# The sparse keys as the last column tile, with the local bias strip in their room and two sets of local rows

## The reference

```python
h = rms_norm(x, ln_attn_pre[l])
mix = hybrid_mixer(h, w_in[l], ...)          # proj = h @ w_in, then three families of heads
x = x + rms_norm(mix @ w_out[l], ln_attn_post[l])
h = rms_norm(x, ln_ffn_pre[l])
f = (jax.nn.silu(h @ ffn_w_gate[l]) * (h @ ffn_w_up[l])) @ ffn_w_down[l]
x = x + rms_norm(f, ln_ffn_post[l])
```

```python
logits = einsum(q, k) / sqrt(d) + bias_tab[t5_bucket(dist)]
p = where(mask, exp(logits - m), 0); out = (p / denom) @ v
```

## Time and profile before

| what | value |
| --- | --- |
| median of 3 runs (lowest to highest) | 1344.51 us (1343.56 to 1347.97) |
| profiled execution | 1344.31 us, its span 1342.4 us |
| mean granted TensorE clock | 0.982 |
| busy over the span | PE 96%, DVE 58%, ACT 41%, POOL 13% |
| DMA | 120.69 MB, mean 90 GB/s |
| value products | to about 72 us |
| first pieces | to about 138 us |
| stick-breaking, local, sparse stage | 138 to 286, to 378, to about 540 us |
| output projection, feed-forward | 549 us to the end |

### The profile page before, as it was taken

One profiled execution on the slowest core, in us unless ns is written; L12 is line 12 of the kernel. 1 busy time (PEld: TensorE's weight loads), 2 busy tenths in 40 slices (PEclk: granted clock), 3 DMA queues, 4 the chain that ended last, 5 costly groups with the idle time before them and its releaser, 6 DMA issues.

```text
span 1342.4 us, 18803 instructions
## 1 busy us (share of the span) xinstructions
PE 1290.8 (96%) x6956; PEld 1104.4 (82%) x6956; DVE 776.7 (58%) x1433; ACT 555.7 (41%) x1044; POOL 177.3 (13%) x162
## 2 busy tenths in 40 slices
PE   7999999989989999799889999999999999999998
PEld 6988788879979999688768888888888778888887
DVE  4342678748757664556856655665566554444455
ACT  4322677747656544433543333333333331121131
POOL 1000000000000000011033323332333100000012
PEclk9999999999989999899989999999999999999999
DMA  7013411134251110522222222212221352332343
GB/s 267 1 46 117 122 48 32 44 105 110 67 130 33 35 62 1 173 94 79 79 79 79 79 86 87 93 64 87 87 94 63 118 181 94 100 103 74 104 153 126
DMA packets 58385, 120.69 MB, mean 90 GB/s; under 512 B 7560, under 2 KB 29328, under 8 KB 58294
## 3 DMA queue, kind: packets, MB, share of 16 engines
q1 hardware_dynamic: 58294, 119.48, 28.4%
HBM read 82.73 MB, written 19.95 MB: 76 GB/s over the span
## 4 chain that ended last, share of the span: by engine, by line
PE 53%; DVE 3%; ACT 1%; issue 1%; POOL 1%; DMA 1%; DVEq 0%; SPq 0%; ACTq 0%; POOLq 0%
PE ps L1975 30%; PE ps L1998 17%; PE ps L1917 5%; PE ps L2135 1%; DVE f_topL L1758 0%; DMA ring<-in_ffn_w_gate 0%; DVE o_tmp L1703 0%; DVE f_W L1764 0%; POOL o_rs L1522 0%; DVE ring L1707 0%; PE ps L1905 0%; DMA ring<-in_ffn_w_up 0%; PE ps L2098 0%; POOL e_tail L2089 0%; ACT o_junk L1563 0%
## 5 line engine op out<-in xcount | busy, mean ns | idle before, releaser
L1975 PE MATMUL ps<-f_topH,f_W 128*128 128x512 f32 x704 | 224.4, 395 | 6.3 <-DVE f_W L1764 4.1
L1975 PEld LDWEIGHTS ps<-f_topH,f_W 128*128 128x128 f32 x704 | 134.3, 191 | 35.7 <-DVE f_W L1764 4.9
L1764 DVE TENSOR_TENSOR f_W<-ring,f_W 128x512 fp32r<-128x512 f32 (+1 forms) x122 | 121.6, 1009 | 51.7 <-ACT f_W L1590 51.7
L1590 ACT CAST f_W<-ring 128x512 fp32r<-128x512 f32 (+1 forms) x122 | 72.4, 595 | 164.9 <-PE ps L1998 153.9
L1975 PE MATMUL ps<-f_topL,f_W 128*128 128x512 f32 x352 | 139.0, 395 | 0.0
L893 PE MATMUL ps<-V,m_tw 128*128 128x66 f32 (+1 forms) x1056 | 130.3, 273 | 0.0
L893 PEld LDWEIGHTS ps<-V,m_tw 128*128 128x128 f32 x1056 | 128.1, 194 | 1.1
L1998 PE MATMUL ps<-f_topH,f_W 128*128 128x512 f32 x448 | 125.0, 390 | 0.0
L1975 PE MATMUL ps<-f_headH,f_W 128*128 128x512 f32 x352 | 115.3, 390 | 1.5 <-DVE f_W L1764 1.5
L1764 DVE TENSOR_TENSOR f_W<-f_scr,f_W 128x512 fp32r<-128x512 f32 x88 | 63.5, 723 | 89.9 <-ACT f_W L1590 89.9
L1880 DVE TENSOR_TENSOR QT<-ps,QT 128x1024 f32<-128x1024 f32 (+1 forms) x48 | 50.2, 1047 | 103.6 <-PE ps L1998 103.6
(11 more groups left out here) (236 smaller groups left out, 2556.4 us busy)
## 6 DMA issues: line engine op xcount, KB each, us to landing
m_qs<-m_qn SPq DMA_DIRECT2D x128, 128.0 KB, 2.4
ring<-in_ffn_w_gate SPq DMA_DIRECT2D x22, 512.0 KB, 4.5
ring<-in_ffn_w_up SPq DMA_DIRECT2D x22, 512.0 KB, 3.6
act_kept<-QT SPq DMA_DIRECT2D x44, 256.0 KB, 2.0
f_scr<-act_kept SPq DMA_DIRECT2D x22, 512.0 KB, 3.5
ring<-in_ffn_w_down SPq DMA_DIRECT2D x32, 256.0 KB, 3.5
ring<-in_w_in_tiles SPq DMA_DIRECT2D x13, 512.0 KB, 3.8
ring<-in_ffn_w_down SPq DMA_DIRECT2D x24, 192.0 KB, 2.4
```

What stands on the lines that cost most here:

```text
L1590: act.copy(slots[s % W_RING][:, 0, 0:n], source(s)).then_inc(hi_done, 1)
L1764: dve.tensor_tensor(slots[s % W_RING][:, 1, 0:n], source(s), slots[s % W_RING][:, 0, 0:n].bitcast(F32), ALU.subtract).then_inc(lo_done, 1)
L1975: ins = pe.matmul(ps[:, bank, :], whole[:, w, cols], halves[h][:, k0 + k, col:col + HALF], start=(begins and k == 0 and w == 0 and h == 0) ...
```

## The change

1. The sparse key tile moves behind the two sparse query tiles and is now the last column tile.
2. `strip_swa` lies in the first half of `KSa`, the room of the sparse keys. Its load has no need in the plan any more; in the code it waits for the compression's products and the value products. The copy of the first half of the sparse key tile waits for the last local logits.
3. `rows_swa` has two sets of rows, by the parity of the token tile, in the room of `rows_sb`. The writers of tiles 0 and 1 wait for the last stick-breaking turn, those of later tiles for the turn of the tile two before.
4. `strip_full` lies in the room of `KSb`. Its three loads wait for the last stick-breaking scores. The gain of the sparse family gets a strip item of its own (4), after the last piece.
5. Sparse logits wait for the last piece, window and selection scores for the key tile's half that they read. Sparse queries need the last query tile only.
6. In `values`, the next tile is turned after step 3 in place of 4.

```diff
@@ -47,7 +47,7 @@
 T_TILES += [("q", 2 + i, [(SQ + 128 * i, 128)]) for i in range(4)]
-T_TILES += [("k", 0, [(KSL, 64), (KW, 64)]), ("q", 0, [(NQ, 128)]), ("q", 1, [(NQ + 128, 128)])]
+T_TILES += [("q", 0, [(NQ, 128)]), ("q", 1, [(NQ + 128, 128)]), ("k", 0, [(KSL, 64), (KW, 64)])]
 NTT = len(T_TILES)
@@ -103,6 +103,7 @@
 GROUPS = 4 * NT
+DB = {"swa": 2}
 FAMILY_WIDTH = {"sb": 256, "swa": 512, "nsa": 256}
@@ -156,7 +157,8 @@
             self.first_row[jobs[j].group] = 4 * j
-        self.same_kind_before = [max((k for k in range(j) if (jobs[k].kind, jobs[k].strip) == (jobs[j].kind, jobs[j].strip)), default=None)
+        self.same_kind_before = [max((k for k in range(j) if jobs[k].n <= jobs[j].n - DB.get(jobs[j].kind, 1)
+                                      and (jobs[k].kind, jobs[k].strip) == (jobs[j].kind, jobs[j].strip)), default=None)
                                  for j in range(self.NJ)]
@@ -219,6 +221,7 @@
 
+    last_swa = ("logits", lay.c_sm[lay.chunk0[4 * (SB_JOBS + SWA_JOBS)]] - 1)
     for i in range(FIRST_LOADS, NTT):
@@ -234,7 +237,8 @@
         if s % 4 == 3:
-            add(("half_keep", h), "act", act(HALF) if kind == "q" else 2 * act(HALF), [("piece", s)], -100)
+            add(("half_keep", h), "act", act(HALF) if kind == "q" else 2 * act(HALF),
+                [("piece", s), last_swa if h == 2 * (NTT - 1) else None], -100)
             if kind == "k":
@@ -248,16 +252,17 @@
 
-    add(("strip", 0), "dma", 7000, [("turn", lay.last_turn(SB_JOBS - 1))], -100)
+    add(("strip", 0), "dma", 7000, [], -100)
     for i in range(1, 4):
-        add(("strip", i), "dma", (0, 5000, 5000, 7000)[i], [("piece", PIECES - 1)], -100)
+        add(("strip", i), "dma", (0, 5000, 5000, 7000)[i], [("scores", lay.chunk0[4 * SB_JOBS] - 1)], -100)
+    add(("strip", 4), "dma", 3000, [("piece", PIECES - 1)], -100)
 
 ...
             half = 1 if job.n >= NT // 2 else 0
-            last_tile = {"sb": 4, "swa": job.q_tile + 5, "nsa": NTT - 1}[job.family]
+            last_tile = {"sb": 4, "swa": job.q_tile + 5, "nsa": NTT - 2}[job.family]
             ready = ("half_keep", 2 * last_tile + half) if 2 * last_tile + half >= FIRST_HALVES else None
@@ -265,13 +270,16 @@
         used = ("turn", lay.last_turn(before)) if before is not None else None
+        if job.family == "swa" and job.n < 2:
+            used = ("turn", lay.last_turn(SB_JOBS - 1))
+        keys = ("half_lo", 2 * (NTT - 1) + (job.n >= NT // 2)) if job.kind in ("win", "slc") else None
         for r in range(4 * j, 4 * j + 4):
 ...
                 w = lay.width(c)
-                add(("scores", c), "pe", 2 * pe(w) + (112 if job.kind in ("sb", "win") else 0), [("spread", g), emptied(c - S_SLOTS)], age - 35)
+                add(("scores", c), "pe", 2 * pe(w) + (112 if job.kind in ("sb", "win") else 0), [("spread", g), emptied(c - S_SLOTS), keys], age - 35)
             if job.kind == "sb":
@@ -286,7 +294,8 @@
                     strip = ("strip", 0) if job.kind == "swa" else ("strip", 1 if job.n < 2 else 2 if job.n < 4 else 3)
-                    add(("logits", lay.c_sm[c]), "dve", dve(w), [("scores", c), used, strip], age)
+                    rows_free = ("piece", PIECES - 1) if job.family == "nsa" else None
+                    add(("logits", lay.c_sm[c]), "dve", dve(w), [("scores", c), used, strip, rows_free], age)
                 add(("softmax", lay.n_sm[r]), "act", act(n, 60), [("logits", lay.c_sm[chunks[-1]])], age + 1)
@@ -413,7 +422,12 @@
             blk = sb("blk", [P, 2, 16, NC_CMP], F32, early)
-        KS = [sb("KSa", [P, 4, S], F32R), sb("KSb", [P, 4, S], F32R)]
+        KSa = sb("KSa", [P, 4, S], F32R)
+        with ExitStack() as early:
+            KSb = sb("KSb", [P, 4, S], F32R, early)
+        strip_full = sb("strip_full", [P, 4, S])
+        KS = [KSa, KSb]
+        strip_swa = KSa[:, 0:2, :].bitcast(F32).rearrange("p a (h l) -> p (a h) l", l=SWA_L)
         identr, mask_sb, mask_win = (sb(n, [P, P], F32R) for n in ("identr", "mask_sb", "mask_win"))
@@ -424,7 +438,7 @@
             rows_sb = sb("rows_sb", [P, 4, S], F32, early)
-        strip_swa, rows_swa = sb("strip_swa", [P, 8, SWA_L]), sb("rows_swa", [P, 8, SWA_L])
+        rows_swa = sb("rows_swa", [P, 2, 8, SWA_L])
 
@@ -453,7 +467,6 @@
             wH, wL = sb("wH", [P, W_ITEMS, HALF], F32R, early), sb("wL", [P, W_ITEMS, HALF], F32R, early)
-        strip_full = sb("strip_full", [P, 4, S])
         rows_nsa = {"slc": sb("rows_slc", [P, 4, S]), "win": sb("rows_win", [P, 4, WIN_BLOCKS * P]), "cmp": sb("rows_cmp", [P, 4, 64])}
@@ -546,7 +559,7 @@
             if job.kind == "swa":
-                return rows_swa[:, i + job.strip, cols]
+                return rows_swa[:, job.n % 2, i + job.strip, cols]
             return rows_nsa[job.kind][:, i, cols]
@@ -565,6 +578,8 @@
                 eng.wait_ge(turned, lay.last_turn(before) + 1)
+            elif jobs[r // 4].kind == "swa":
+                eng.wait_ge(turned, lay.last_turn(SB_JOBS - 1) + 1)
 
@@ -660,17 +675,20 @@
                         sp.dma_start(g_w[:], bass.AP(grp_g.tensor, 256, [[0, P], [1, 512]])).then_inc(gains_in[1], 16)
-                        sp.wait_ge(turned, lay.last_turn(SB_JOBS - 1) + 1)
+                        sp.wait_ge(phi_done, NPHI)
+                        sp.wait_ge(v_done, NT)
                         sp.wait_ge(tab_out, 32)
-                        sp.dma_start(strip_swa[:], bass.AP(table_swa.tensor, 0, [[1, P], [SWA_T, 8], [1, SWA_L]])).then_inc(strips_in[0], 16)
+                        sp.dma_start(strip_swa, bass.AP(table_swa.tensor, 0, [[1, P], [SWA_T, 8], [1, SWA_L]])).then_inc(strips_in[0], 16)
+                    elif i == 4:
+                        sp.wait_ge(piece_done, PIECES)
+                        sp.dma_start(g_n[:], bass.AP(grp_g.tensor, 0, [[0, P], [1, 256]])).then_inc(gains_in[2], 16)
                     else:
 ...
                         if i == 1:
-                            sp.wait_ge(piece_done, PIECES)
+                            sp.wait_ge(tab_out, 32)
+                            sp.wait_ge(scores_ready, chunk0[4 * SB_JOBS])
                         sp.dma_start(strip_full[:, :, c0:c1],
                                      bass.AP(table_full.tensor, c0, [[1, P], [FULL_T, 4], [1, c1 - c0]])).then_inc(strips_in[i], 16)
-                        if i == 1:
-                            sp.dma_start(g_n[:], bass.AP(grp_g.tensor, 0, [[0, P], [1, 256]])).then_inc(gains_in[2], 16)
 
@@ -736,7 +754,7 @@
                                                 start=(k == 0 and h is hH and w == 0), stop=(k == KT - 1 and h is hL))
-                        if k == 4 and t + 1 < NT:
+                        if k == 3 and t + 1 < NT:
                             turn_x(t + 1)
@@ -815,8 +833,8 @@
                             pe.wait_ge(half_lo_done, lo_before(2 * 5 + 2))
-                        else:
-                            pe.wait_ge(half_lo_done, lo_before(HALVES))
+                    if job.kind in ("win", "slc"):
+                        pe.wait_ge(half_lo_done, lo_before(HALVES) - (job.n < NT // 2))
                     if c < S_SLOTS:
@@ -933,6 +951,8 @@
                     act.wait_ge(piece_done, 4 * h + 4)
+                    if h == 2 * (NTT - 1):
+                        act.wait_ge(neg_ready, c_sm[chunk0[4 * (SB_JOBS + SWA_JOBS)]])
                     hf, src = h % 2, ps[:, half_bank(h), :]
@@ -1184,6 +1204,8 @@
                         minus_sink()
+                    if job.family == "nsa":
+                        dve.wait_ge(piece_done, PIECES)
                     dve.wait_ge(strips_in[0 if job.kind == "swa" else 1 if job.n < 2 else 2 if job.n < 4 else 3], 16)
```

## The result

The changed kernel takes 1349.53 us (median) beside 1345.29 us for the kernel before: ratio 1.0028 (95%: 1.0017 to 1.0038). A second comparison gave 1348.04 beside 1346.53 us, ratio 1.0011 (0.9997 to 1.0025). So the change costs 1.5 to 4.2 us where the forecast was -5.2, and both medians lie above the range. The second interval takes in no change; that the kernel is slower at all rests on the first. The profiled execution's span is 1346.5 us (1342.4 before).

A forecast was written before the change was run, and what follows sets the result against it. TensorE, busy 96% of the span, was taken as the bound, so only its idle time and low clock could go. Terms -2.4 + 4.4 - 4.3 + 2.0 - 3.1 - 1.8 = -5.2 us took 1344.31 to 1339.1 us, range 1333.5 to 1345.5.

The forecast's parts named there:

- Value products: Value products: turning the next tile one step earlier removes six waits of 0.40 us, -2.4 us (bounds -1.2 and -3.3).
- Front of the SyncE queue: Before stick-breaking: gain and strip delay the first spread 3.8 us, plus 0.6 of low clock, +4.4 us.
- upper bound of +5.4: Upper bound of the front-of-queue term, with up to 1.5 us more for low clock; its lower bound was 0.
- The delay of 2.7 us: First spread's delay if strip and spread were served side by side, sharing the DMA engines, instead of in ring order.
- Stick-breaking to local: Start of the local stage: the 2.8 us idle and 1.5 us of low clock behind it go, -4.3 us.
- the last rival: Near 291 us: the strip's move alone brings nothing, the tile order closes the gap; within the forecast, no chance given.
- The double rows: Local stage: two sets of rows costed at nothing, since VectorE waited for scores before it wrote a row.
- Sparse key tile at the end: End of the local stage: the wait between key halves comes back half covered, +2.0 us (bounds 0 and +4.3).
- Start of the sparse stage: First sparse logits: 0.6 of 3.7 us idle stays, -3.1 us, with a further -1.8 us for the clock.
- The clock's part (-1.8): Start of the sparse stage: less low clock after the shorter idle time, -1.8 us, taken between 0 and -4.2.
- To the end of the kernel: Stages after the sparse one: they keep their work and their order; no term in the sum.
- The rival "given back": Whole kernel: front costs 5.4, key gap uncovered at 4.3, sparse start's clock stays low; 1344.2 us, chance 0.25.

The follow-up runs named there:

- 2: Kernel before the change with only the turn of the next tile after step 3 in place of 4: ratio 0.9983 to the kernel before.
- run 1: Changed kernel with the local strip and gain loads moved from the queue's front to behind the first five spreads: ratio 0.9986 to the kernel before.
- run 3: Kernel before with only the local gain and an unread copy of the 1 MB strip loaded ahead of the first spread: ratio 1.0065, +8.8 us.
- run 8: Changed kernel with gain and strip behind the third spread and the key tile's first half early: 1335.02 and 1335.40 us, ratios 0.9928 and 0.9931 to before.
- 5: Changed kernel with only half of the strip and the gain ahead of the first spread, the other half behind four stick-breaking jobs: ratio 1.0007 to before.
- 6: Changed kernel with one set of local rows in place of two: ratio 1.0021 to the kernel before.
- run 9: Kernel before with only the order of the column tiles changed (sparse keys last), strips and local rows where they were: ratio 0.9994 to the kernel before.
- 4: Changed kernel with 16 unread matmuls of 512 columns on TensorE while it waits for the first spread: ratio 1.0003 to the kernel before.
- run 7: On top of run 1, four pieces of the sparse key tile's first half run ahead of the last local weighings: ratio 0.9953 to the kernel before.

## Why the prediction was wrong

**Value products**: -2.7 us for the forecast -2.4, alone -2.3 us by the ratio of 2. Right.

**Front of the SyncE queue**: the delay is right (4.2 for 3.8 us). The low clock behind it is the step that failed. The text put it at 0.6, "since this stage has 9.3 us of TensorE idle to take some of it", with a bound of 1.5 taken from a shorter wait. It measured 3.3 us (second profile), 6.0 with the second stretch (first profile), and the stage's idle time took hardly any of it: that is 6.2 us in the profiles with and without low clock. By the profiles the term is 3.8 + 3.3 = +7.1 to 4.2 + 6.0 = +10.2 in place of +4.4, and its upper bound of +5.4 (3.8 and 1.5 make 5.3) was no bound. The medians bracket this widely: taking the front away brought 3.4 to 5.6 us (run 1), adding it cost 8.8 (run 3). The second stretch can't be put down to the front, since it comes in kernels without the wait too. Fifteen profiles sort this out, two each of the changed kernel and of the one of run 8: the five with the wait (3.1 to 4.5 us: the two of the changed kernel, 3, 5 and 6) all have the low stretch behind it and 116.1 to 118.9 us of scores; the ten without it or with fillers have 112.8 to 112.9 (six) or 116.0 to 116.3 (four, those with the stretch at 164). The mistake in method was to price it by the shorter of two examples: 2.8 us of idle time had been followed by 3.4 us at half clock, but the earlier trace rows also have 3.70 us followed by 8.6 us at 0.51, which is 4.2 us lost. Here 4.5 us came with 6.8. The Trainium skill, page "TensorE: Matmul & The Clock Gate", section "What's actually happening", says that the low clock is the default state and that activity lifts it; the fillers' windows agree.

On the bytes, the Trainium skill's rule of ring order (page "DMA: Bandwidth & Descriptors", section "Queues, rings and completion order") is borne out: spread behind strip comes 4.2 us late, behind half of it 2.8, behind none 0. The delay of 2.7 us that the prediction gives for a shared service isn't what the whole strip shows.

**Stick-breaking to local**: the idle time went as forecast. The 1.5 us of clock were credited from one profile; two profiles that keep the 2.8 us wait (2 and 3) show no low clock behind it, so the sure part is -2.8. No term has what grew beside it: with idle time and the time lost to low clock taken off, the stretch from the last stick-breaking turn to the last piece is 89.8 us before, 90.0 and 90.2 in runs 2 and 3, but 91.2 in run 9 and 91.0 to 91.1 in the changed kernel. So about 1.2 us go with the order of the tiles; that is why the table has +1.1 for this stretch. Run 9 shows that the wait belongs to that order, as the last rival says. The double rows cost and bring nothing, as costed.

**Sparse key tile at the end**: the second step that failed, in size. +2.0 was forecast, +4.3 came in both profiles of the changed kernel (2.8 idle, and 1.5 to 1.6 of clock behind it; runs 4 and 6 have the same wait and no low clock behind it): the copy of its first half (376.5) found no turns or weighings left, with 8 pieces behind the last local logits for 6 before. The bound of +4.3 was just met. Run 9 shows the cover where the copy may come early, run 7 that four pieces moved ahead of the last weighings bring it back.

**Start of the sparse stage**: 4.7 + 158.5 us became 0.6 + 156.8, so -5.8 for the forecast -4.9. Idle time at the start fell by 3.2 us (forecast 3.1): right. The clock's part (-1.8) came out well partly by luck. From the last piece to the last weighing it takes 157.4 us in both profiles of the changed kernel, but 155.7 to 163.0 in the nine others with this start, with 1.7 to 10.2 us lost to low clock (before: 163.2, with 7.6 lost).

**To the end of the kernel**: +1.5 us with no edit. From the first product of the output projection to TensorE's last matmul it takes 788.0 us in both profiles of the changed kernel, 788.1 before; the difference lies behind that matmul, 6.3 us for 4.7. The two profiles of the one kernel of run 8 have 6.3 and 4.7 there too, so the same code shows both values and nothing ties them to the change.

By the table, the first profile of the changed kernel is -2.7 + 4.2 + 6.0 - 0.2 + 1.1 - 5.8 + 1.5 = +4.1 us beside that of the kernel before, the second -4.0 + 3.8 + 3.3 - 0.2 + 1.2 - 5.8 + 1.5 = -0.2, where the medians say +4.2 and +1.5. The second was the fastest of its 12 runs, so this account holds for the executions profiled and is no proof of the medians. The rival "given back" had this mechanism, with 5.4 for the front; with 7.1 there it would have stood at 1345.9, just past the range. Undoing the front gave 0.9986, and covering the key tile as well 0.9953.

## What to carry to other kernels

A wait of TensorE ahead of a dense stage can cost nearly twice its length (here 3.8 us of delay and 3.3 of low clock): count the stretch of low clock behind it in full, and take away no idle time of the stage for it. Ask of each load without a need where in the issuing queue it will stand and which small, urgent transfer stands behind it; here one edge in the plan (run 1 against the changed kernel) is worth 3.4 to 5.6 us by the medians. A tile that inherits another's room also inherits the date of its last reader, so look whether the work that used to cover its waits is still there at that date.

## What had not been expected of the hardware

- A second low stretch between 164 and 181 appears in eight of fifteen profiles, with much the same idle time ahead of it as where it stays away (2.1 to 2.2 of 4 us busy where it is least, no single wait over 1.6 us) and no transfer awaited, and in two kernels, the changed one and that of run 8, it came in one profile and not in the other. A difference of 3.4 us between two single profiles can be just that.
- Seven of the fifteen profiles have a low stretch of 3.4 us that begins between 64 and 68 us, at the end of the value products, though in that of run 1 TensorE had been busy without a pause from 54 us on. Neither profile of the changed kernel has it, one of run 8's two does.
- Sixteen fillers (3.89 us) in the wait at the front kept the clock at 1.00; without them half clock held for 6.8 us.
